# Moving eight expert rows per layer into an earlier stretch, and re-spacing the gathered rows behind them

## The reference, cut to what matters

```
def peer(x, wq, keys, u_tab, v_tab):          # x: tokens x 1024, tables: 16384 x 1024
    q = x @ wq                                # 8 heads, two halves of 64 each
    s = q . keys                              # 128 scores per head and half
    ... top 16 of each half, top 16 of their 256 sums -> e (expert numbers), gate = softmax
    act = gelu(einsum('td,thkd->thk', x, u_tab[e]))
    return einsum('thk,thkd->td', gate * act, v_tab[e])

    h = h + peer(rmsnorm(h))
    h = h + sigmoid(rmsnorm(h) @ w_gate) * (p @ w_ple)
```

## Time and profile before

| | |
|---|---|
| median of 3 runs | 4024.82 us (4018.37 to 4047.0) |
| the profiled execution's own time | 4042.12 us |
| span of its trace | 4040.3 us |
| mean granted TensorE clock | 0.98 of full |
| PE busy | 3890.4 us (96%) |
| DVE, ACT, POOL busy | 2873.7, 1536.6, 2332.6 us (71%, 38%, 58%) |
| DMA | 900.99 MB, 223 GB/s over the span |

### The profile page before, as it was taken

How to read it: one execution, slowest core, us unless ns; L and a number is a source line. 1 busy time by engine, 2 the same in 40 slices (tenths; PEclk the granted TensorE clock), 3 DMA queues, 4 the chain that set the end, 5 groups by cost and what they waited for, 6 DMA issues and landing times.

```text
span 4040.3 us, 59456 instructions
## 1 busy us (share of the span) xinstructions
PE 3890.4 (96%) x23204; PEld 3471.2 (86%) x23204; DVE 2873.7 (71%) x4841; ACT 1536.6 (38%) x2353; POOL 2332.6 (58%) x1452
## 2 busy tenths in 40 slices
PE   8999999999999999999999999999999999999998
PEld 6788599999999999989477786999999999998983
DVE  5764369955888778788467652699468887788874
ACT  1443145453333333333314432555433333443333
POOL 0122068887877568888001320788877774788770
PEclk9988999999999999999999799999999999999999
DMA  4201146666989999999222011566679999999981
GB/s 121 52 13 48 43 170 221 204 230 225 323 305 326 339 345 381 376 364 340 70 65 39 12 69 47 180 212 211 218 247 322 312 323 341 347 381 366 385 294 54
DMA packets 417975, 900.99 MB, mean 223 GB/s; under 512 B 94496, under 2 KB 242208, under 8 KB 416032
## 3 DMA queue, kind: packets, MB, share of 16 engines
q1 hardware_dynamic: 272288, 552.91, 40.4%
q0 software_dynamic: 90112, 268.76, 18.5%
q10 hardware_dynamic: 55296, 75.52, 5.1%
HBM read 773.87 MB, written 123.15 MB: 222 GB/s over the span
## 4 chain that ended last, share of the span: by engine, by line
PE 57%; POOL 19%; DVE 11%; DMA 6%; issue 5%; ACT 2%; SPq 0%; DVEq 0%; ACTq 0%; POOLq 0%
PE banks L1369 22%; POOL u_stage L2100 9%; POOL peer_gates L2084 8%; PE banks L831 7%; PE banks L1381 6%; PE banks L1280 3%; PE banks L1478 3%; PE banks L1424 3%; PE banks L1298 3%; DMA u_stage<-peer_ut 3%; DMA peer_gates<-peer_v,u_stage 2%; PE banks L1137 1%; PE banks L1124 1%; DMA gated<-dense_gelus 1%; PE banks L914 1%
## 5 line engine op out<-in xcount | busy, mean ns | idle before, releaser
L1443 PE MATMUL banks<-gated_parts,v_parts 128*128 128x320 f32 x6144 | 923.6, 312 | 60.5 <-DVE gated_parts L2783 58.7
L1443 PEld LDWEIGHTS banks<-gated_parts,v_parts 128*128 128x128 f32 x6144 | 910.1, 189 | 74.3 <-issue 73.8
L2084 POOL DMA_INDIRECT peer_gates<-peer_v,u_stage x512 | 767.9, 1500 | 329.7 <-DVE normed L2734 138.0
L1369 PE MATMUL banks<-peer_x_parts,u_parts 128*128 128x448 f32 x3168 | 662.5, 366 | 0.8 <-DVE u_parts L2720 0.8
L1369 PEld LDWEIGHTS banks<-peer_x_parts,u_parts 128*128 128x128 f32 x3168 | 590.1, 188 | 45.9 <-DVE u_parts L2720 1.2
L2100 POOL DMA_INDIRECT u_stage<-dense_gelus,u_stage x256 | 403.9, 1578 | 104.5 <-issue 77.4
L2750 DVE SCALAR_TENSOR_TENSOR peer_gates<-peer_gates,u_stage 128x1024 f32<-128x1024 f32 x254 | 325.9, 1283 | 144.3 <-DMA peer_gates<-peer_v,u_stage 118.5
L1369 PE MATMUL banks<-peer_x_parts,low_s 128*128 128x448 f32 x1696 | 396.9, 366 | 0.0
L2092 POOL DMA_INDIRECT u_stage<-gelus,u_stage x256 | 338.6, 1323 | 78.0 <-issue 77.9
L2077 POOL TENSOR_TENSOR parts_a<-x,parts_a 128x1024 fp32r<-128x1024 f32 x64 | 170.4, 2683 | 365.2 <-ACT parts_a L1823 365.2
L1874 ACT ACTIVATE u_stage<-banks 128x448 f32<-128x448 f32 x256 | 139.2, 544 | 636.1 <-PE banks L1369 619.8
(11 more groups left out here) (355 smaller groups left out, 6655.2 us busy)
## 6 DMA issues: line engine op xcount, KB each, us to landing
v_stage<-peer_v SPq DMA_DIRECT2D x256, 512.0 KB, 6.9
u_stage<-peer_ut SPq DMA_DIRECT2D x244, 512.0 KB, 5.2
dense_gelus<-u_stage ACTq DMA_DIRECT2D x256, 224.0 KB, 5.4
gates<-peer_gates SPq DMA_DIRECT2D x16, 2560.0 KB, 17.5
u_stage<-gates SPq DMA_DIRECT2D x64, 640.0 KB, 8.0
gated<-dense_gelus SPq DMA_DIRECT2D x256, 160.0 KB, 5.4
x<-peer_ut SPq DMA_DIRECT2D x64, 512.0 KB, 4.8
u_raw<-peer_ut SPq DMA_DIRECT2D x64, 512.0 KB, 4.9
```

What stands on the lines that cost most here:

```text
L1369: ins = mm(PS[:, d % 2, 0:DW], u_part(n, a, k), XR[:, b, k, DENSE0:TOK], start=(k == 0 and m == 0), stop=(k == KT - 1 and m == 2))
L1443: ins = mm(vc[k][:, 0:PW3], VR[:, s, b, k * 128:(k + 1) * 128], HR[:, s, a, :], start=(j == 0 and m == 0), stop=(j == NKEYS - 1 and m == 2))
L2084: eng.indirect_dma_start(out=GU[:, t % 4, :], out_offset=None, in_=din["peer_v"].rearrange("l i j d -> (l i j) d"), in_offset=bass.Indirec ...
```

## The change

- `FIRST_ROWS` takes rows with r % 8 in (0, 3, 6): 48 rows in place of 40 are dense in the first stretch, and 80 in place of 88 are loaded again later. `B_ROWS` ends in 1: each block of 5 units has 9 dense rows in place of 10. The tail steps stay at 8.
- All 128 natural slots are added in the units and tail steps; the four late ones in the V stage are gone. The first four picked rows are gathered in their place ahead of the wait for the stored gelu values.
- Picked slot m is added in V row 8 + m * 25 // 24: from row 8 on, 24 slots in each 25 rows, 115 in the stage (before: 118). 13 slots are left for the tail (before: 10). They are added as 3, 5 and 5, and their sum is used one half tile of PLE later.
- On PE the turn of tile 2 comes before the transposes of the half tile, the turns of tiles 3 and SAMPLE come one or two PLE halves later, and `turn(SAMPLE)` now stands right before `turn(3 * L + 3, 0)`. ACT and DVE are reordered to match.

```
-FIRST_ROWS = [r for r in range(NKEYS) if r % 16 in (0, 3, 6, 9, 12)]
+FIRST_ROWS = [r for r in range(NKEYS) if r % 8 in (0, 3, 6)]
-GV = 4
-LATE_FROM = 6
-B_ROWS = [2, 2, 2, 2, 2]
+B_ROWS = [2, 2, 2, 2, 1]
-PICKED = 10
+PICKED = 8
-TAIL_SLOTS = range(NKEYS - PICKED, SLOTS)
+IN_PASS = 24 * (NKEYS - PICKED) // 25
+TAIL_SLOTS = range(IN_PASS, SLOTS)
     def slots_of_step(g):
-        each, last = GSLOTS - GV, SLOT_AT[-1]
+        each, last = GSLOTS, SLOT_AT[-1]
-    def late_slots_of_row(j):
-        return [GSLOTS - GV + m for m in range(GV) if LATE_FROM + m * 3 // 2 == j]
     def slots_of_row(j):
-        return [j - PICKED] if j >= PICKED else []
+        return [m for m in range(IN_PASS) if PICKED + m * 25 // 24 == j]
...
# TensorE, tail
             ple_half(0, 1)
+            turn(3 * L + 2, 2)
             down_turned(2)
-            turn(3 * L + 2, 2)
             ple_half(1, 0)
+            ple_half(1, 1)
+            ple_half(2, 0)
             turn(3 * L + 2, 3)
-            ple_half(1, 1)
+            ple_half(2, 1)
             turn(3 * L + 2, SAMPLE)
-            ple_half(2, 0)
-            ple_half(2, 1)
             if L + 1 < DEPTH:
                 turn(3 * L + 3, 0)
...
# GpSimd, behind the units
-            for m in range(4):
-                gather_row(GSLOTS - GV + m)
+            for s in range(4):
+                gather_row(GSLOTS + s)
             ... wait for the stored gelu values, then 12 gather_weight
-            for s in range(SLOTS):
+            for s in range(4, SLOTS):
                 gather_row(GSLOTS + s)
-                gather_weight(s + WEIGHTS_AHEAD)
+                gather_weight(s - 4 + WEIGHTS_AHEAD)
...
# VectorE: row j of the V stage
-                for m in late_slots_of_row(j):
-                    add_natural(m)
...
# VectorE, tail
             scale(3 * L + 2, 2)
-            for m in TAIL_SLOTS[3:]:
+            for m in TAIL_SLOTS[3:8]:
                 add_picked(m)
             ple_half(0, 1)
+            turned(3 * L + 2, 2)
+            for m in TAIL_SLOTS[8:]:
+                add_picked(m)
+            ple_half(1, 0)
             picked_done()
             add_down(SPLIT)
-            turned(3 * L + 2, 2)
             scale(3 * L + 2, 3)
-            ple_half(1, 0)
+            ple_half(1, 1)
+            scale(3 * L + 2, SAMPLE)
+            ple_half(2, 0)
             turned(3 * L + 2, 3)
-            scale(3 * L + 2, SAMPLE)
-            ple_half(1, 1)
+            next_scale(0)
+            ple_half(2, 1)
             turned(3 * L + 2, SAMPLE)
-            next_scale(0)
-            ple_half(2, 0)
             next_scale(1)
-            ple_half(2, 1)
```

More of the change, by code:

```diff
@@ L1979, in _ @@
             sigmoid(0, 1)
+            sigmoid(1, 0)
             rms(3 * L + 2, 3)
-            sigmoid(1, 0)
+            sigmoid(1, 1)
             rms(3 * L + 2, SAMPLE)
-            sigmoid(1, 1)
+            sigmoid(2, 0)
             rms(3 * L + 3, 0)
-            sigmoid(2, 0)
+            sigmoid(2, 1)
             rms(3 * L + 3, 1)
-            sigmoid(2, 1)
             rms(3 * L + 3, 2)
```

## The result

The changed kernel takes 4074.89 us (median of 4 runs, 4060.12 to 4101.27), the kernel before 4028.48 in the same session (4018.37 to 4047.0): a ratio of 1.0132, 95% interval 1.0092 to 1.0173. It is 1.3% slower, where 0.8% faster was forecast; rival 1 had named 4070 us.

What follows compares the result with a forecast made beforehand. PE, busy 3890.4 of 4040.3 us, was taken as the bound, with POOL pacing the V stage. Terms -27 - 5 + 14 - 13.6 = -31.6 took the profiled 4042.1 to 4010.5; median forecast 3993 us, 8 in 10 range 3955 to 4030.

Steps and rivals of the forecast that it cites:

- rival 1: Units: POOL standing still behind each block's 2560 KB store costs 42 us a layer; kernel slower, at 4070 us; chance 0.05.
- The units, "14 us lost": Units of both layers: shorter blocks with more slots make POOL the bound, costing 7 us a layer.
- POOL becomes the bound by 2.0 us a block: Units: POOL needs 54.6 us in a block of 52.6, for some 6.4 blocks until the values run out.
- nearly gone: Units: sign expected in the profile, that POOL's waits for DVE, so far 67.9 us, almost vanish.
- standstill of 4.5 us a block: Units, within rival 1: POOL stands still behind the gate store, so a block needs 60.2 us, 7.6 over.
- The V stage, "27 us gained": V stage: twelve fewer POOL instructions until the last slot gain 15 us in layer 0, 12 in layer 1.
- rival 2: V stage: a dropped slot gives back its whole price, 22.9 us a layer; kernel at 3974 us; chance 0.27.
- First stretch, "5 us gained": First stretch: six dense rows in eight pairs end PE's 4.9 us of waits for POOL's low parts.
- The tail, "13.6 us gained": Tail: later turns close PE's stops of 6.67 and 6.61 us; net 5.6 us in layer 0, 8.0 in layer 1.
- The sum: Whole kernel: V stage, first stretch, units and tail together, -27 - 5 + 14 - 13.6 = -31.6 us.

## Why the prediction was wrong

**The units, "14 us lost": measured 93.** This is the step that failed; all others together were off by less. The terms of the mean were fair: a slot cost POOL 3.34 us (1413 and 1325 ns and twice 0.30) against the 3.41 used. What failed is the balance over a block. "POOL becomes the bound by 2.0 us a block" supposes that POOL works without a stop and that being late by 2 us costs 2. The runs showed three other things.

- POOL can't use all of its time. It stopped for DVE for 67 us before and after (the forecast was "nearly gone"), since DVE takes rows three or four at a time from four buffers, and a row needs 6.8 us to land. A fifth buffer took 34 us of DVE's waits away in layer 0 and 0.8% of the time, with the store in pieces 1.5%. How exactly it helps is argued: POOL's own stops stayed at 72.6 us.
- The gate store makes rows of u late. In the units of layer 0 before, ACT waits for one behind each of the eight stores, 2.5 to 7.1 us; after, behind six of them, up to 11.9. That a two-row unit hides such a wait and a one-row unit doesn't fits PE's waits, 2.1 us before and 30.1 after, but no run shows it by itself.
- Behind a wait of some us PE works at the lower clock, 17 us for 30 us of waits. The forecast left this out here, though it had counted the same effect in the tail.

The two-row units could absorb nearly all of this (4.2 and 6.7 us of waits for one-hots with the rows back and one store); taking 4.86 us out of each block used up the slack at a threshold, which half the value gathers and four smaller stores together bring back.

**Rival 1 was the case, in the main.** It gave 42 us a layer and 4070 us; measured 45 and 48, and 4075. Its mechanism, the burst of the store on top of POOL without slack, is borne out by the kernels with one cause removed (20 and 27 us) and both (88). Its number is in part luck: its standstill of 4.5 us a block was measured in no run, it left out the clock, and by its own sum the profiled execution would take 4087 us and not 4060. Its evidence against itself, that POOL waits 67.9 us for DVE, was misread: that idle time was not slack, for it stayed while PE's waits grew. It got 0.05 on that ground.

**The V stage, "27 us gained": 52 in the pair.** Fourteen profiled kernels with this V stage take 456 to 482 us in a layer, mean 470.4; two with the old one 488.8 to 493.8, mean 491.7. So 21.3 us a layer, 43 in all: the size of rival 2 (22.9 a layer). Whether its price for a slot is the reason isn't shown; no run changed the number of picked slots alone. PE's waits for gated parts went to 21.4 us (forecast: about 30). POOL's busy time fell by 39 us in layer 0, more than eight instructions, since a gather's mean fell from 1620 to 1495 ns; and POOL now waits for DVE 33.8 us (before 2.6). That TENSOR_TENSORs which fall into those waits hold up nothing is argued, not shown. The rule of the Trainium skill (SBUF — State Buffer, section "SBUF: two separate sides") named beside that rival still has the row against it: the gather beside the adds at 1298.46 takes 0.96 us.

**First stretch, "5 us gained": 7.1.** PE's two waits for POOL's low parts (2.7 and 2.2 us) are gone, as forecast, but not for the reason forecast. With the old rows back, five in eight pairs, they are gone as well and the stretch takes 385.6 us; from there to 424.3 are the 38.7 us of eight dense rows. The right number was luck, and what ends these waits stays open.

**The tail, "13.6 us gained": right in mechanism.** The gap of 6.67 closed and the new wait of 3.83 came (3.8 forecast). Layer 1 gained 8.3 (8.0 forecast). Layer 0 can't be told from the mixer in the table; from the end of the V stage to the next mixer's first matmul it was 4.2 (5.6 forecast). The turn itself starts 5.8 us sooner, and the slow matmuls behind the new wait, which the forecast left out, take the rest back.

**The sum.** -52 - 7 + 93 - 13 and what the untouched mixers varied (-3) make the +18 of the profiles. The other 28 us between that and the medians are where the two profiled executions lie: 15 us under the median after, 14 above it before. In which stages they arise stays open.

## What to carry to other kernels

Work that is moved out of a stage takes its slack along: before you cut the time that PE gives a block, list what the longer block hides (late loads behind a big store, a producer that feeds a short ring in bursts) and ask for each whether it fits into the shortest step, not into the mean. Idle time of a producer in a ring isn't spare capacity when its consumer takes in bursts; add a buffer before you count on it. Work that the bounding engine has to do in either place gains nothing by being moved, so the most to be won is what waits disappear. And where removing one suspect gives only a part, remove two at a time: here 20 and 27 us alone, 88 together.

## What the runs showed of the hardware

- **A wait of some us is paid again in clock, a shorter one often isn't.** Behind a wait of 5.09 us the 16 one-hot products took 3.78 us in place of 1.95. In the kernel with five buffers they took 2.05 behind waits of 0.53 and 2.13 us, but 2.81 behind one of 2.01.
- **A gathered row lands long after its instruction has ended.** POOL's indirect DMA of 128 rows of 4 KB takes 0.94 us, or 1.96 beside DVE's TENSOR_TENSORs, but it lands 6.8 us (4.5 to 10.0) after its issue.
- **A stretch in which PE gets its matmuls one by one.** In several executions, some 35 to 65 us into the units, PE shows "issue" gaps of about 1 us between single matmuls with no semaphore behind them. From the kernel with five buffers, old rows and the store in pieces, layer 0:

```profile
978.46 0.73 PE L1388 MATMUL banks<-peer_x_parts,u_parts 128*128 128x448 f32 x1 [1.03 <-issue]
979.86 0.53 PE L1388 MATMUL banks<-peer_x_parts,u_parts 128*128 128x448 f32 x1 [0.67 <-issue]
...
974.00:992.00 18.00, 10.23 (x22) 6.00 (x22) 6.73 (x6) 2.27 (x4) 11.79 (x11) 0.52 0.68 221
```

  In the 18 us from 974 the granted clock was 0.52 and DMA moved 221 GB/s; as far into the units of the kernel before (from 979) it was 1.00 and 362 GB/s. The units of that kernel took 517.5 us without any wait for another engine, in place of 503, so it costs about 14 us. It came with the one-row unit in the middle, with the rows back (store whole and in pieces) and in all three with five buffers, not in the other eleven profiles, and may explain some of the spread between runs of one kernel. Its cause is open.
